# Taking out the 512-byte rounding ahead of the weight ring in SBUF, and moving seven small tiles behind it

## The reference

```
proj = x @ w_in                       # 1024 x 8208, split in ten parts
y_a  = rms_norm(gla_chunked(q_a, k_a, v_a, decay)) * silu(r_a)
y_b  = moba_attention(rope(q_b), rope(k_b), v_b)      # 8 heads
x    = layer_norm(alpha*x + (sigmoid(gate_a)*y_a + sigmoid(gate_b)*y_b) @ w_out)
s    = (x @ w_q) . sub_keys           # 8 heads, two halves, 128 keys each
expert, gate = top 16 of 16 x 16 sums per head, softmax
hid  = gelu(x . u_tab[expert]);  h = sum(gate * hid * v_tab[expert])
x    = layer_norm(alpha*x + h)
```

## Time and profile before

| | |
|---|---|
| three runs | 1124.44, 1124.57, 1126.77 us; median 1124.57 us |
| the profiled execution | 1124.57 us |
| its span, first to last instruction | 1122.7 us, so 1.9 us lie around it |
| PE busy | 1080.5 us, 96% of the span |
| DVE / POOL / ACT busy | 811.5 / 580.7 / 554.9 us |
| granted TensorE clock, mean | 0.991 of full speed |
| moved by DMA | 186.5 MB |

### The profile page before, as it was taken

How to read it: one execution, slowest core, us unless ns; L and a number is a source line. 1 busy time by engine, 2 the same in 40 slices (tenths; PEclk the granted TensorE clock), 3 DMA queues, 4 the chain that set the end, 5 groups by cost and what they waited for, 6 DMA issues and landing times.

```text
span 1122.7 us, 20715 instructions
## 1 busy us (share of the span) xinstructions
PE 1080.5 (96%) x6734; PEld 967.1 (86%) x6734; DVE 811.5 (72%) x1398; ACT 554.9 (49%) x898; POOL 580.7 (52%) x452
## 2 busy tenths in 40 slices
PE   6999999995999999999989999999999999999995
PEld 4887888675999999999989999998888888888884
DVE  4347656375799978888997788986666666666666
ACT  4347544542445455554545545555545545544542
POOL 4484345434222246656555666755555555555554
PEclk9999999997999999999999999999999999999998
DMA  6654344242445454444443443446555555555552
GB/s 202 242 188 164 136 153 148 97 166 73 154 167 177 172 178 155 164 155 163 149 149 144 150 139 135 146 142 217 199 190 188 197 194 188 197 195 187 194 198 95
DMA packets 52473, 186.51 MB, mean 166 GB/s; under 512 B 6208, under 2 KB 6592, under 8 KB 52432
## 3 DMA queue, kind: packets, MB, share of 16 engines
q1 hardware_dynamic: 51584, 182.87, 46.4%
q0 software_dynamic: 848, 3.15, 0.8%
HBM read 184.94 MB, written 1.05 MB: 166 GB/s over the span
## 4 chain that ended last, share of the span: by engine, by line
PE 85%; DVE 8%; DMA 2%; issue 1%; POOL 1%; ACT 1%; DVEq 0%; SPq 0%; POOLq 0%
PE ps L1151 16%; PE ps L1153 15%; PE ps L1152 15%; PE ps L1451 10%; PE ps L1452 10%; PE ps L1453 10%; PE ps L1411 5%; DVE wlo L718 2%; PE ps L1191 1%; DMA raw<-w_tiles_in 1%; DVE hot L1025 1%; POOL wlo L347 1%; DVE sel L1030 1%; ACT whi L483 1%; PE ps L1378 1%
## 5 line engine op out<-in xcount | busy, mean ns | idle before, releaser
L347 POOL TENSOR_TENSOR wlo<-raw,whi 128x256 fp32r<-128x256 f32 x341 | 432.3, 1269 | 491.4 <-ACT whi L483 490.6
L718 DVE TENSOR_TENSOR wlo<-raw,whi 128x768 fp32r<-128x768 f32 x341 | 357.4, 1049 | 247.1 <-ACT whi L483 245.3
L483 ACT ACTIVATE whi<-raw 128x1024 fp32r<-128x1024 f32 x344 | 364.4, 1060 | 320.8 <-DMA raw<-w_tiles_v 171.0
L1151 PE MATMUL ps<-ahi,whi 128*128 128x256 f32 x1152 | 333.5, 290 | 2.7 <-DVE alo L965 1.4
L1153 PE MATMUL ps<-ahi,wlo 128*128 128x256 f32 x1152 | 326.3, 283 | 0.0
L1152 PE MATMUL ps<-alo,whi 128*128 128x256 f32 x1152 | 326.3, 283 | 0.0
L1151 PEld LDWEIGHTS ps<-ahi,whi 128*128 128x128 f32 x1152 | 221.3, 192 | 3.6 <-DVE alo L965 1.8
L1152 PEld LDWEIGHTS ps<-alo,whi 128*128 128x128 f32 x1152 | 221.5, 192 | 0.0
L1153 PEld LDWEIGHTS ps<-ahi,wlo 128*128 128x128 f32 x1152 | 221.1, 192 | 0.0
L1451 PE MATMUL ps<-whi,hhi 128*128 128x512 f32 x512 | 199.3, 389 | 1.8 <-POOL wlo L347 1.8
L1452 PE MATMUL ps<-wlo,hhi 128*128 128x512 f32 x512 | 199.2, 389 | 0.0
(11 more groups left out here) (190 smaller groups left out, 998.1 us busy)
## 6 DMA issues: line engine op xcount, KB each, us to landing
raw<-w_tiles_u SPq DMA_DIRECT2D x128, 512.0 KB, 3.2
raw<-w_tiles_v SPq DMA_DIRECT2D x128, 512.0 KB, 3.2
raw<-w_tiles_in SPq DMA_DIRECT2D x64, 512.0 KB, 3.3
raw<-w_tiles_q SPq DMA_DIRECT2D x16, 512.0 KB, 3.2
raw<-w_tiles_out SPq DMA_DIRECT2D x8, 512.0 KB, 3.3
xraw<-xT SPq DMA_DIRECT2D x4, 256.0 KB, 5.9
xt<-x POOLq DMA_DIRECT2D x1, 1024.0 KB, 5.4
out<-xt SPq DMA_DIRECT2D x4, 256.0 KB, 2.0
```

Source lines behind the costliest of these rows:

```text
L347: pool.tensor_tensor(wlo[:, tile.slot, DVE_COLS:], raw[:, tile.slot, DVE_COLS:], whi[:, tile.slot, DVE_COLS:].bitcast(F32), ALU.subtract)\
L483: act.activation(whi[:, tile.slot, :], raw[:, tile.slot, :], ACT.Copy)\
L718: dve.tensor_tensor(wlo[:, tile.slot, 0:DVE_COLS], raw[:, tile.slot, 0:DVE_COLS], whi[:, tile.slot, 0:DVE_COLS].bitcast(F32), ALU.subtract)\
L1151: pe.matmul(out, ah, bh, start=start, stop=False)
```

## The change

No instruction, no semaphore and no order changes; only addresses in SBUF do. Before, `ident`, `keys`, `stats`, `mv`, `rstd`, `shift` and `gate_warm` lie ahead of the ring, and the ring's start is rounded up to a multiple of 512. After, the ring starts at the first free byte and the seven tiles lie behind `xt` (with `iota` between `keys` and `stats`).

```diff
-    ident = place("ident", [P, P])
-    keys = place("keys", [P, 2, NK])
-    stats = place("stats", [P, NT, 2, 6])
-    mv = place("mv", [P, NT, 2])
-    rstd = place("rstd", [P, NT])
-    shift = place("shift", [P, 1])
-    gate_warm = place("gate_warm", [P, 1])
-    at[0] = (at[0] + 511) // 512 * 512
     ring_at = at[0]
     raw = place("raw", [P, NS, W])
     wlo = place("wlo", [P, NS, W], F32R, alias=ring_at)
...
     xt = place("xt", [P, NT, D])
+    ident = place("ident", [P, P])
+    keys = place("keys", [P, 2, NK])
     iota = place("iota", [P, P])
+    stats = place("stats", [P, NT, 2, 6])
+    mv = place("mv", [P, NT, 2])
+    rstd = place("rstd", [P, NT])
+    shift = place("shift", [P, 1])
+    gate_warm = place("gate_warm", [P, 1])
     work_at = at[0]
```

## The result

The changed kernel takes 1133.49 us (median of six runs, 1133.14 to 1137.83) against 1125.21 for the kernel before (six runs). The ratio is 1.0081, with a 95% interval of 1.0069 to 1.0093: slower by 0.8%, outside the forecast range. The span of the profiled execution went from 1122.7 to 1132.8 us, by 10.1.

The account below looks back on a forecast made before the run. PE was taken to bound the kernel, busy 1080.5 of 1122.7 us. Terms: 1124.6 + 0.2 (ring loads) + 0 + 0 + 0 = 1124.8 us; range 1123.0 to 1127.2, its end extended to 1127.5.

Parts of the forecast that it names:

- What bounds the kernel: Whole kernel: PE, busy 1080.5 of 1122.7 us, sets the time wherever nothing makes it wait.
- the cost of *PE: PE's matmul operands at shifted addresses: value 0, bounds 0 and +0.3 us.
- the cover: `v_tab` stage: weight loads of `hhi`, `hlo`, 188 ns beneath a matmul each 226.5, hide up to 38 ns.
- Rival B: PE pays for the offset, one 0.42 ns cycle on each of 6734 matmuls: 2.8 us, 1127.4 us; chance 0.04.
- Rival C: Faster, old layout collides with other engines' accesses: 6.8 us back over 1536 matmuls, 1117.8 us; chance 0.07 including a small reshuffle.
- The DMA terms: Ring loads 0.03 us slower each, +0.2 us, at most +2.1; other transfers 0, at most +0.1.
- the seven places of the chain: Seven loads, from the first tile to the last of `v_tab`, in the chain that ended last; slower loads cost there.
- Rival A: Ring writes off a boundary are slow: 1129.1 us at packets 1.5 times as long, 1169 at 2; chance 0.09.
- 17 transactions for 16: Ring loads off a 256-byte boundary: 0.08 us more each, 0.6 for seven, 1125.2 us.
- ACT, DVE, POOL: These engines' operations on moved tiles: value 0, at most 0.1 us where DVE leads a gate block.
- The sum: Whole kernel: 1124.6 + 0.2 + 0 + 0 + 0 = 1124.8 us; 1127.2 with all upper bounds.
- The chance of 0.13 for slower: Whole kernel slower beyond about 0.2%, 2.25 us: rivals A (0.09) and B (0.04); same 0.80, faster 0.07.

Follow-up runs that it names:

- The still-weights pair: Kernel before, `v_tab` weights from a once-filled tile, no product with `H`: tile 32 past a multiple of 256, 1136.14 us; `hhi`, `hlo` 32 past instead, 1123.30 us.
- four profiles on one chip: Kernel before with all work tiles 32 up (1135.21 us), `hhi`/`hlo` 32 up (1134.64), ring alone 128 up (1134.69); changed kernel with work tiles on multiples of 64 (1126.58).
- the mended kernel: Changed kernel with the work tiles' start rounded up to a multiple of 64, the ring still at 128: 1126.58 us, ratio 1.0002.
- the run with the second pair: Kernel before plus `ahi2`, `alo2`, 32 bytes above `ahi`, `alo`, serving only the queries and the `u_tab` stage: 1117.84 us, ratio 0.9931.

## Why the prediction was wrong, point by point

**What bounds the kernel: right.** PE sets the time, and the whole loss is PE's. In the `v_tab` stage it shows in no wait at all.

**The step that failed is the cost of *PE*: "value 0", with bounds "0 and +0.3".** It measured +10.0 us: 1536 x (232.8 - 226.3), by the counts from 860 to 1080 us. Three things went wrong in it. First, it asked what each tile's own address costs, and looked for rows of a tile 128 or 32 past a boundary. The run with everything 32 up shows that this costs nothing measurable (ratio 1.0006, 0.9993 to 1.0020). What costs is the distance between the two tiles of one matmul, which the change altered for `hhi` and `hlo` and the table of addresses ahead of the prediction had in plain sight: 128 for the ring, 352 for them. Second, the rows taken as evidence, 275 and 274 ns for 128 columns, were durations, not the spacing of starts, and of matmuls of 128 columns. In this case 6.7 ns in the spacing were 6 in the duration, but the row `L1450 PEld` didn't move at all (188 to 187). Third, the cover: "a matmul each 226.5, which hides up to 38 ns" took for granted that the weight load and the moving data of the matmul under way don't disturb each other. The still-weights pair, with its last 24 matmuls at 233.5 and 227 ns, shows that they do.

The Trainium skill ("TensorE: Matmul & The Clock Gate", section "Step-by-step: what each phase is for") calls TensorE's two SBUF read ports, for `rhs` and for the weights, independent. As far as this means that one read doesn't slow the other, the measurement decides against it: 226.3 or 233.1 ns by the distance alone.

**Rival B** had the right side, and its price was too low: "one cycle of 0.42 ns" for each of 6734 matmuls, 2.8 us, where 6.5 ns on 1536 were lost. Its sign of being right, fewer matmuls in the 270 us, is what came: 1158 for 1192. **Rival C** looked for two accesses that meet, as was the case, but between PE and other engines, and in the old layout, which is the fast one for 512 columns; the 13.2 ns beyond 213.3 that it named "have no cause that the trace names" still have none. For 256 columns a gain by address does exist: 2.4 ns a matmul at a distance of 224.

**The DMA terms: right, as far as can be told.** +0.2 us was forecast for the seven places of the chain, with +2.1 at most. The changed kernel with its distance mended keeps the ring at 128 and has a ratio of 1.0002 (0.9988 to 1.0015), so at most 1.7 us; 0.2 can't be told from nothing. A packet took 0.485 x 16 x 1132.8 / 51,584 = 0.170 us in the changed kernel and 0.491 x 16 x 1123.0 / 51,584 = 0.171 in the second profile of the kernel before, and 0.170 in each of the four profiles on one chip. Rival A is refuted. The Trainium skill's rule that the prediction quotes ("DMA: Bandwidth & Descriptors", section "How a descriptor splits into AXI transactions"), priced as there by 17 transactions for 16, would have made packets 6% longer; no such lengthening shows here.

**ACT, DVE, POOL: right.** Value 0, and the run with everything 32 up shows no loss beyond its interval. DVE's and POOL's busy times rose, from 811.5 to 815.5 and from 580.7 to 589.1 us, but the kernel before has 812.9 and 586.3 in its second profile.

**The sum and the chances.** Without PE's loss the forecast holds: 1124.8 for 1124.6 is a ratio of 1.0002, and the mended kernel has 1.0002 (0.9988 to 1.0015). The chance of 0.13 for slower was small because an unmeasured pair of operands was costed by single ones.

## What to carry to other kernels

When an edit moves tiles, tabulate for each matmul in a bound stage the distance of its two operands modulo 256, before and after, and not the alignment of each. Compare the spacing of starts (count in a fully busy stretch), not mean durations. A layout chosen per stage, by an alias some bytes off, was worth 0.7% here without a further instruction; and before a small shift in a DMA share is believed, profile the unchanged kernel twice.

## What the runs showed of the hardware that was not expected

- The spacing of back-to-back float32r matmuls depends on the distance between the SBUF addresses of weights and moving data, modulo 256: at 512 columns 226.3 ns at 0 and 231.8 to 233.8 at 32, 64, 96, 128 and 224. That it is modulo 256 and not 512 rests on the mended kernel, at 256 modulo 512 and fast, and on `alo` at 256 in the run with the second pair, whose input projection stayed fast (447 matmuls for 445).
- At 256 columns 0, 128 and 160 are alike (122.7 to 122.8 ns), and 224, 192 and 32 faster, at 120.3, 120.7 and 121.5 ns. The sign counts. The values at 32, 160 and 192 rest on one run each.
- At 512 columns it is PE's reads of weights and of moving data that disturb each other: 233.5 against 227.0 ns a start with still weights and with nobody writing the ring. Where they meet wasn't measured, nor why the long matmuls like 0 best and the short ones 224, nor whether for the short ones other engines take part.
- The share of time of the same DMA packets was 46.4% in one profile of the kernel before and 49.1% in the other, without effect on the span (1122.7 and 1123.0 us).
